# Sixty-four-row products for two panels of the last gate of a two-layer decoder trunk

## What is computed

```python
h = h + rms_norm(f, ln_ffn_post[i])
gate = jax.nn.sigmoid(h @ ple_w_gate[i] + ple_b_gate[i])   # 256x2048 times 2048x2048
h = h + gate * (p[i] @ ple_w_proj[i])
```

## Time and profile before

| | |
|---|---|
| median of 3 runs | 2439.1 us (2436.96 to 2439.43) |
| the profiled execution's own time | 2439.21 us |
| its span, first to last instruction | 2437.5 us |
| TensorE matmul busy | 2406.7 us, 99% of the span |
| TensorE weight loads busy | 2010.2 us, 82% |
| VectorE busy | 1458.1 us, 60% |
| ScalarE busy | 1047.1 us, 43% |
| DMA | 448.97 MB, mean 184 GB/s |
| granted TensorE clock, mean | 0.999 |

### The profile page before, as it was taken

The page is one execution under the profiler, slowest core; times in us unless marked ns, Lnnn a source line. Parts: engine busy times, 40 slices in busy tenths (PEclk is TensorE's granted clock), DMA queues, the critical chain, the costliest instruction groups (busy, mean ns, idle before and its releaser), DMA issues.

```text
span 2437.5 us, 29420 instructions
## 1 busy us (share of the span) xinstructions
PE 2406.7 (99%) x11688; PEld 2010.2 (82%) x11688; DVE 1458.1 (60%) x1476; ACT 1047.1 (43%) x1003; POOL 20.5 (1%) x38
## 2 busy tenths in 40 slices
PE   7999999999999999999999999999999999999999
PEld 7887888888888888888888888888888888888887
DVE  4654656664466545657676677566654666457575
ACT  4444445443333433345544355463443433334453
POOL 0000100000000000000000000000000000000000
PEclk9999999999999999999999999999999999999999
DMA  7554556655556556546555633466556555565464
GB/s 224 179 175 130 174 174 210 194 197 191 193 190 191 189 196 196 175 173 224 190 186 178 212 119 107 143 207 191 194 191 197 192 189 190 192 198 188 169 220 138
DMA packets 226962, 448.97 MB, mean 184 GB/s; under 512 B 7961, under 2 KB 19233, under 8 KB 225586
## 3 DMA queue, kind: packets, MB, share of 16 engines
q1 hardware_dynamic: 225218, 440.72, 55.3%
q10 hardware_dynamic: 1648, 6.89, 0.8%
HBM read 445.48 MB, written 2.10 MB: 184 GB/s over the span
## 4 chain that ended last, share of the span: by engine, by line
PE 96%; DVE 2%; ACT 1%; issue 0%; DMA 0%; ACTq 0%; DVEq 0%
PE PG L540 89%; PE MB L540 1%; PE MB L871 1%; PE MB L663 1%; PE MB L643 1%; PE MB L673 0%; ACT whl L1049 0%; PE MB L524 0%; DVE whl L1467 0%; PE MB L641 0%; PE MB L645 0%; PE MB L682 0%; PE PG L584 0%; PE PG L585 0%; PE PG L586 0%
## 5 line engine op out<-in xcount | busy, mean ns | idle before, releaser
L1467 DVE TENSOR_TENSOR whl<-raw,whl 128x2048 fp32r<-128x2048 f32 (+4 forms) x435 | 955.8, 2198 | 810.6 <-ACT whl L1049 810.5
L1049 ACT ACTIVATE whl<-raw 128x2048 fp32r<-128x2048 f32 (+4 forms) x435 | 800.9, 1841 | 1165.4 <-PE PG L540 1149.8
L540 PE MATMUL PG<-whl,XBh 128*128 128x512 f32 (+1 forms) x3376 | 797.3, 386 | 1.7 <-ACT XBh L1057 0.8
L540 PE MATMUL PG<-whl,XAh 128*128 128x512 f32 (+1 forms) x3136 | 743.9, 387 | 3.1 <-ACT whl L1049 2.2
L540 PEld LDWEIGHTS PG<-whl,XBh 128*128 128x128 f32 x3376 | 624.8, 188 | 128.2 <-issue 1.7
L540 PEld LDWEIGHTS PG<-whl,XAh 128*128 128x128 f32 x3136 | 584.9, 188 | 120.2 <-issue 3.1
L540 PE MATMUL PG<-whl,XBl 128*128 128x512 f32 (+1 forms) x1688 | 412.4, 386 | 0.0
L540 PE MATMUL PG<-whl,XAl 128*128 128x512 f32 (+1 forms) x1568 | 383.5, 386 | 0.0
L540 PEld LDWEIGHTS PG<-whl,XBl 128*128 128x128 f32 x1688 | 313.2, 188 | 63.0
L540 PEld LDWEIGHTS PG<-whl,XAl 128*128 128x128 f32 x1568 | 292.1, 188 | 57.1
L2031 DVE STREAM_TRANSPOSE HT<-Hb 32x256 f32<-32x256 f32 x256 | 111.6, 436 | 4.1
(11 more groups left out here) (339 smaller groups left out, 1019.2 us busy)
## 6 DMA issues: line engine op xcount, KB each, us to landing
raw<-in_ffn_w_gate SPq DMA_DIRECT2D x88, 1024.0 KB, 5.2
raw<-in_ffn_w_up SPq DMA_DIRECT2D x88, 1024.0 KB, 5.1
raw<-in_ffn_w_down SPq DMA_DIRECT2D x64, 1024.0 KB, 5.0
raw<-in_nsa_w_in SPq DMA_DIRECT2D x36, 1024.0 KB, 5.1
raw<-in_ple_w_gate SPq DMA_DIRECT2D x32, 1024.0 KB, 5.0
raw<-in_ab_w_in SPq DMA_DIRECT2D x24, 1024.0 KB, 5.3
raw<-in_ffn_w_down SPq DMA_DIRECT2D x32, 768.0 KB, 4.3
raw<-in_ab_w_out SPq DMA_DIRECT2D x16, 1024.0 KB, 5.1
```

The source lines that it names most:

```text
L540: return mm(bank(m), X[x][:, chunk, m * P:(m + 1) * P], w[:, k, c * ncol:(c + 1) * ncol], start=x == 0 and w is wh and c == 0 and pos in ( ...
L1049: A(wh[:, place % 2, 0:w], raw[:, place, 0:w], ACT.Copy).then_inc(hi_ready, 1)
L1467: V.tensor_tensor(wl[:, k, 0:w], raw[:, place, 0:w], wh[:, k, 0:w].bitcast(F32), ALU.subtract).then_inc(lo_ready, 1)
```

## The change

A new function `unit_rows` on TensorE takes the place of `unit` for the eight units of the slots `GATE[1] + 1` and `GATE[1] + 2`; the four units of `GATE[1] + 3` stay as they are. Each 128-row product is cut into one over the upper 64 rows and one over the lower 64 rows, issued one behind the other, the upper into the bank of one half of the tokens and the lower into the bank of the other half. In the first turn of a unit the upper rows go to bank `j % 2` and the lower to the other; then comes a `pstep`, and in the second turn the two are exchanged. The two turns together cover what `unit` covers. The next unit begins with the banks that the last one ended with.

```diff
+            def unit_rows(s, j, X, par):
+                pe.wait_ge(hi_ready, U(s) + (j + 1))
+                k = U.place(s, j) % 2
+                for turn in range(2):
+                    for x, w in ((0, wh), (1, wh), (0, wl)):
+                        if w is wl:
+                            pe.wait_ge(lo_ready, U(s) + (j + 1))
+                        for c in range(4):
+                            for r in range(2):
+                                m, rr = (r + turn + j) % 2, slice(64 * r, 64 * r + 64)
+                                last = mm(PG[:, par, m, :], X[x][rr, 4 * j + c, m * P:(m + 1) * P],
+                                          w[rr, k, c * 512:(c + 1) * 512],
+                                          start=turn == 0 and x == 0 and w is wh and c == 0 and j == 0,
+                                          stop=turn == 1 and w is wl and c == 3 and j == 3)
+                    if turn == 0:
+                        pstep(last)
+                last.then_inc(unit_done, 1)
...
                         for j in range(4):
-                            unit(s, j, XIN[1], half=(s, j) == (GATE[1] + 3, 3))
+                            if s < GATE[1] + 3:
+                                unit_rows(s, j, XIN[1], s % 2)
+                            else:
+                                unit(s, j, XIN[1], half=(s, j) == (GATE[1] + 3, 3))
```

## The result

The changed kernel takes 2442.16 us, median of 20 runs (2440.35 to 2442.94); the kernel before, run beside it, 2438.79 us (2436.61 to 2439.77, 20 runs). The ratio is 1.0015, 95% interval 1.0009 to 1.0021: 3.4 us more, within the 0.2% that was called no change, and on the slow side as forecast (+3.3 us). The profiled execution took 2442.76 us, its span is 2441.0 us, 3.5 us more than before.

A forecast was written before the change was run, and what follows sets the result against it. TensorE, its matmuls busy for 99% of the span, was taken to bound the kernel. Waits 2.9, row changes 0.4 and pairs 0 gave +3.3 us on the profiled 2439.2: 2442.5 us, range 2438.2 to 2446.0.

The forecast's parts named there:

- The pairs: Upper and lower 64-row products in the eight units run together at a full-row product's beat, 0.2267 us; 0 us over 192 pairs.
- One fixed part a pair: Each pair's beat pays the 0.012 us not due to columns once, staying at 0.2267 us; chance 0.50.
- the fixed part gone: Rival: pairs in the eight units lose the beat's 12 ns not due to columns; -2.3 us, total 2440.2 us; chance 0.27.
- doubled: Rival: each member of a pair pays the 0.012 us, beat 0.2387 us; +2.3 us, total 2444.8 us; chance 0.08.
- No overlap: Rival: in fp32r the lower product follows the upper instead of running beside it; 43.5 us more, 2486.0 us; chance 0.10.
- exposed loads: Rival: each of 192 pairs waits 0.11 us for its own weight load; 21.1 us more, 2463.6 us; chance 0.03.
- The pstep: One wait of TensorE on itself per unit, eight in all, 0.35 to 0.36 us each; +2.9 us.
- The two pieces taken from other lines: Cost of each unit's `pstep`: +0.24 us for the drain, +0.11 us for the weight load no longer hidden.
- The change-overs: Going to 64 rows ahead of `GATE[1] + 1` (0.20 us) and back ahead of `GATE[1] + 3` (0.21 us); +0.4 us.
- The sum: Whole kernel: 2.9 + 0.4 + 0 = +3.3 us on the profiled 2439.2 us, giving 2442.5 us.
- The moved waits and the clock: `lo_ready`, awaited 1.8 us into a unit instead of 3.6, costs 0; the clock in the two panels stays at 1.00.
- The signs that were named: Expected in the two panels' timeline: 0.227 us pair beat, 5.8 us units, 46.8 us between `gate_add` marks, no `lo_ready` wait.

The follow-up runs named there:

- e1: Changed kernel without the bank exchange and its eight waits, each row half keeping its bank; 2439.15 us, ratio 1.0002 to the kernel before.
- e6: Changed kernel with each product cut in four over 32 rows into four fixed banks, no wait; 2438.76 us, ratio 1.0001 to the kernel before.
- e5: Changed kernel without exchange and wait, the middle part of each unit done with full-row products; 2441.42 us, ratio 1.0015 to the kernel before.
- e4: Changed kernel with products reordered, four over the upper rows, then four over the lower, same banks; 2443.66 us, ratio 1.0022 to the kernel before.
- e10: Kernel before with 64-row products in blocks of four per row half, no exchange or wait, `lo_ready` awaited at unit start; 2439.64 us, ratio 1.0004.

## Why the prediction was right

**The pairs.** The forecast rested on float32 pairs lasting no longer than full-row products. In fp32r it is the same to the hundredth: 21.76 us a panel in e1 as before. "One fixed part a pair" held. Had the fixed part gone or doubled, the panel would have been 96 x 0.012 = 1.2 us shorter or longer; e1 rules out both, and e6 the same for groups of four. No overlap (10 us a unit) and exposed loads (8.4) fall by the 5.81 us of the changed kernel.

**The pstep.** 0.36 us was said, 0.3725 measured, 0.3525 with full rows. The two pieces taken from other lines held, if not to the last digit: +0.22 for the drain against 0.24 from the earlier trace rows, +0.11 for the load. What the sum lacked is a third piece, some beats behind each restart that are up to 0.01 us too long, 0.04 us in a changed unit. The piece that was 0.02 too dear and the one that was missing partly cancel, so the sum came out nearer than its parts; that is luck.

**The change-overs.** 0.4 us was said for the two, 0.49 measured. In e5 the first product of the other kind starts 0.32 us after the last of the old one, and the next 0.34 after that: 0.09 and 0.11 over a beat, as it was read from the earlier trace rows. The same third piece is missing there: the six beats that follow a change to full rows are up to 0.236 us.

**The sum.** 2.9 + 0.4 = 3.3 against 3.0 + 0.5 = 3.5 in the profiled span and 3.4 in the medians. The interval of the ratio is 2.2 to 5.1 us, so the time alone shows only that the cost is small; it is the panels that bear out the terms.

**The moved waits and the clock.** No wait for `lo_ready` or `hi_ready` appears, as forecast. ScalarE's splits start 0.37 us a unit later, and this delayed nothing. The signs that were named came as well: 2413.45 - 2366.70 = 46.75 us from one `gate_add` to the one two panels on (46.8 was said), and the clock at 1.00. The idle stretch of the loads is 0.49 us, 0.4 was said.

**Exposed loads.** The prediction gave them 0.03, because in the earlier trace rows a load of all rows runs beside a matmul of all rows. A unit of 5.81 us, not 8.4, decides for the row.

Not settled: why the beats behind a restart are uneven and why row halves have more of them; what the reach of four places counts (products, their loads, or something that fills up), whether it is another at other widths, and whether a semaphore on the last product of such a queue still covers those ahead of it. Blocks of four cost 0.15 us a unit in e4, where a wait stops the unit while one row half is 0.13 us behind, and only 0.23 us once in the whole of e10, where nothing stops them; that this lag is the cause is read from the traces and was not tested alone. Two row halves into the same bank at once were not tried, and nothing here shows whether their sums would come out right.

No variant beat the kernel before. Row halves hold the beat of full rows at best, so the wait and the change-overs have nothing to be paid from. A version with more banks instead of the exchange was not built; as an estimate from e1, it would still be 0.5 us behind, and it would have to add the banks up as well.

## What to carry to other kernels

Cutting a full 128-row product into row tiles gained nothing here: with fp32r and 512 moving columns the beat is 0.2267 us, whether one, two or four products share it. So row tiles are for rows that are short anyway. In such a stream count each wait of TensorE on itself as 0.35 to 0.37 us and each change between full rows and 64-row products as 0.23 to 0.26 us. To price a wait, add three things: the product's latency (and some 0.06 us more) in place of a beat, the weight load that is no longer hidden, and a few long beats behind it.

## What was not expected of the hardware

Products of different row halves are started out of the queue's order, from four places behind the one that they join, in all five block lengths. With blocks of four or six over one half and then the other, a unit takes about as long as with alternating pairs (5.44 and 5.50 us against 5.44). Longer blocks save 3.3 to 3.4 beats at each border, and each product beyond them takes a beat of its own (6.26 us at eight, 7.83 at twelve, 9.38 at 24). And four 32-row fp32r products go in one beat of 0.2267 us just as two of 64 rows or one of 128.
